# First block of a two-block model: norm statistics as rows from products with ones, and the first projections side by side

## The reference

```python
def rms_norm(x, g):
    xf = x.astype(jnp.float32)
    y = xf * lax.rsqrt(jnp.mean(xf * xf, axis=-1, keepdims=True) + EPS)
    return (y * g.astype(jnp.float32)).astype(x.dtype)

    for l in range(DEPTH):
        z = rms_norm(h, norm_g[l])
...
    zp = jnp.einsum('btd,de->bte', z, w_in)
```

## Time and profile before

| | us |
|---|---|
| median of 3 runs (lowest, highest) | 1664.25 (1663.14, 1668.55) |
| profiled execution, whole | 1667.13 |
| its span | 1665.3 |
| PE busy in it | 1588.7 |
| DVE busy | 1139.6 |
| ACT busy | 899.4 |
| mean granted clock of PE | 0.984 |

### The profile page before, as it was taken

How to read it: one execution, slowest core, us unless ns; L and a number is a source line. 1 busy time by engine, 2 the same in 40 slices (tenths; PEclk the granted TensorE clock), 3 DMA queues, 4 the chain that set the end, 5 groups by cost and what they waited for, 6 DMA issues and landing times.

```text
span 1665.3 us, 32288 instructions
## 1 busy us (share of the span) xinstructions
PE 1588.7 (95%) x12500; PEld 1539.7 (92%) x12500; DVE 1139.6 (68%) x1727; ACT 899.4 (54%) x1423; POOL 48.9 (3%) x60
## 2 busy tenths in 40 slices
PE   7989999997989999999999999999999999999996
PEld 7977899886888999999999999999999899999996
DVE  4875677458768766677877766676666786776666
ACT  5644565378665544467555544464445755464443
POOL 0000000000000000002100000000000030000000
PEclk9989999899999999999999999999999999999998
DMA  5433223544443655545445655556555544556554
GB/s 196 132 101 99 64 77 118 174 140 127 144 140 109 197 184 187 189 152 169 148 148 169 201 181 186 189 168 199 183 184 174 158 159 140 189 164 192 185 182 136
DMA packets 73314, 263.66 MB, mean 158 GB/s; under 512 B 8144, under 2 KB 9680, under 8 KB 73104
## 3 DMA queue, kind: packets, MB, share of 16 engines
q1 hardware_dynamic: 70560, 252.66, 47.4%
q0 software_dynamic: 2672, 9.86, 1.8%
HBM read 261.43 MB, written 1.05 MB: 158 GB/s over the span
## 4 chain that ended last, share of the span: by engine, by line
PE 82%; DVE 9%; ACT 5%; issue 2%; DMA 2%; DVEq 0%; SPq 0%; ACTq 0%
PE PS L1490 24%; PE PS L1492 23%; PE PS L1491 23%; DVE w_lo L944 3%; PE PS L1733 2%; PE PS L1676 1%; PE PS L1838 1%; DMA raw<-stream 1%; ACT w_hi L489 1%; DVE zf L1269 1%; PE PS L1501 1%; PE PS L1749 1%; PE PS L1666 1%; PE PS L1652 1%; ACT work L855 1%
## 5 line engine op out<-in xcount | busy, mean ns | idle before, releaser
L1490 PE MATMUL PS<-YH,w_hi 128*128 128x256 f32 (+1 forms) x2812 | 815.2, 290 | 19.0 <-DVE YL L1430 8.3
L1492 PE MATMUL PS<-YH,w_lo 128*128 128x256 f32 (+1 forms) x2812 | 799.9, 284 | 0.0
L1491 PE MATMUL PS<-YL,w_hi 128*128 128x256 f32 (+1 forms) x2812 | 799.5, 284 | 0.0
L944 DVE TENSOR_TENSOR w_lo<-raw,w_hi 128x1024 fp32r<-128x1024 f32 x476 | 585.6, 1233 | 167.2 <-ACT w_hi L489 163.9
L1490 PEld LDWEIGHTS PS<-YH,w_hi 128*128 128x128 f32 x2812 | 535.7, 191 | 27.3 <-issue 10.3
L489 ACT ACTIVATE w_hi<-raw 128x1024 fp32r<-128x1024 f32 x476 | 499.5, 1052 | 99.3 <-PE PS L1492 53.5
L1491 PEld LDWEIGHTS PS<-YL,w_hi 128*128 128x128 f32 x2812 | 535.7, 191 | 2.5 <-issue 0.5
L1492 PEld LDWEIGHTS PS<-YH,w_lo 128*128 128x128 f32 x2812 | 536.9, 191 | 0.0
L1490 PE MATMUL PS<-hH,w_hi 128*128 128x256 f32 x832 | 233.3, 280 | 6.4 <-DVE hL L1037 6.4
L1491 PE MATMUL PS<-hL,w_hi 128*128 128x256 f32 x832 | 233.3, 280 | 0.0
L1492 PE MATMUL PS<-hH,w_lo 128*128 128x256 f32 x832 | 233.3, 280 | 0.0
(11 more groups left out here) (296 smaller groups left out, 1414.8 us busy)
## 6 DMA issues: line engine op xcount, KB each, us to landing
raw<-stream SPq DMA_DIRECT2D x476, 512.0 KB, 4.1
work<-stream POOLq DMA_DIRECT2D x16, 512.0 KB, 4.1
X<-x SPq DMA_DIRECT2D x1, 1088.0 KB, 5.0
out<-zf SPq DMA_DIRECT2D x8, 128.0 KB, 2.0
work<-rope SPq DMA_DIRECT2D x1, 544.0 KB, 7.7
work<-levels POOLq DMA_DIRECT2D x1, 512.0 KB, 3.9
work<-inv_count POOLq DMA_DIRECT2D x1, 512.0 KB, 4.6
work<-band POOLq DMA_DIRECT2D x1, 408.0 KB, 4.6
```

The source lines that it names most:

```text
L944: dve.tensor_tensor(w_lo[:, s.slot, :], raw[:, s.slot % RAW, :], f32(w_hi[:, s.slot, :]), ALU.subtract).then_inc(lo_ready, 1)
L1490: pe.matmul(to, wh, xh, start=start, stop=False, skip_group_check=True)
L1491: pe.matmul(to, wh, xl, start=False, stop=False, skip_group_check=True)
L1492: return pe.matmul(to, wl, xh, start=False, stop=stop, skip_group_check=True)
```

## The change

In both norms of the first block, PE sums with ones as the stationary operand (128 x 128) and the squares as the moving one: 8 products of 272 columns, and every partition of bank 6 holds the row of sums. ACT takes the root straight from PSUM over 272 columns, with scale and epsilon in the same operation; DVE takes the reciprocal over 272 columns in `rsf`. The step of scale and epsilon, the diagonal and the spreading are gone. The dummy root stands ahead of the squares (at the start also ahead of the wait for x, and behind a new wait for the constants, since the root reads epsilon). At the start three slabs are split instead of two (`FIRST = 3`); ACT does its splits behind the root, and DVE does its own behind the reciprocal and ahead of the first `zf`, no longer ahead of the norm.

PE takes the first slabs side by side (`beside`): it waits for the last of them to be split, and then, chunk by chunk, issues the three matmuls of the chunk for each slab in its own bank. That holds for slabs 0 to 2 of the even layer and for the four `u` slabs of the odd layer's first group. `from_z` loses its wait for `zL`; its callers drop the argument.

```diff
--- before.py
+++ after.py
@@ -27,7 +27,7 @@
 RAW = 3
 LEAD = 4
 
-FIRST = 2
+FIRST = 3
 SLAB = 8 * P
 
 FF = 2816 // P
@@ -194,8 +194,7 @@
         hH = sb("hH", [P, 2, T1], F32R)
         hL = sb("hL", [P, 2, T1], F32R)
 
-        rs = sb("rs", [P, 3])
-        diag = sb("diag", [P, 3 * 96])
+        rsf = sb("rsf", [P, T1])
         ident = sb("ident", [P, P])
         C = sb("C", [P, ncols])
         ones = sb("ones", [P, P])
...
@@ -489,18 +483,18 @@
                 act.activation(w_hi[:, s.slot, :], raw[:, s.slot % RAW, :], ACT.Copy).then_inc(hi_ready, 1)
 
             def norm(v, xr, T, xo):
+                act.activation(warm[:, 1:2], warm[:, 0:1], ACT.Sqrt)
+                if xr is None:
+                    act.wait_ge(x_loaded, 16)
                 for c in range(DC):
                     if xr is not None:
                         act.wait_ge(x_ready, xr + c // 2 + 1)
                     act.activation(zf[:, c, 0:T], X[:, c, xo:xo + T], ACT.Square).then_inc(sq_ready, 1)
+                act.wait_ge(ssq_ready, v + 1)
+                act.activation(rsf[:, 0:T], PS[:, 6, 0:T], ACT.Sqrt, bias=eps_col, scale=1.0 / D).then_inc(root_ready, 1)
                 if xr is None:
                     for k in range(FIRST):
                         split(Slab(0, k))
-
-                act.activation(warm[:, 1:2], warm[:, 0:1], ACT.Sqrt)
-                act.wait_ge(ms_ready, v + 1)
-                w, n = tiles(T)
-                act.activation(rs[0:w, 0:n], rs[0:w, 0:n], ACT.Sqrt).then_inc(root_ready, 1)
 
             def norm_hi(v, T):
                 for c in range(DC):
@@ -914,7 +908,7 @@
                             split(odd(o_out(g - 1) + 3 + LEAD))
 
             act.wait_ge(warm_ready, 1)
-            act.wait_ge(x_loaded, 16)
+            act.wait_ge(consts, 4)
             norm(0, None, T1, 0)
             norm_hi(0, T1)
             for k in range(FIRST, LEAD):
@@ -945,15 +939,11 @@
                                   ALU.subtract).then_inc(lo_ready, 1)
 
             def norm(v, xr, T, xo, col):
-                dve.wait_ge(ssq_ready, v + 1)
-                w, n = tiles(T)
-                dve.tensor_scalar(rs[0:w, 0:n], PS[0:w, 6, 0:n], 1.0 / D, EPS, ALU.mult, ALU.add).then_inc(ms_ready, 1)
                 dve.wait_ge(root_ready, v + 1)
-                step.step(dve.reciprocal(rs[0:w, 0:n], rs[0:w, 0:n]))
-                dg = diag[0:w, 0:n * w].rearrange("p (n t) -> p n t", t=w)
-                dve.tensor_tensor(dg, ident[0:w, None, 0:w].to_broadcast([w, n, w]), rs[0:w, 0:n, None].to_broadcast([w, n, w]),
-                                  ALU.mult).then_inc(diag_ready, 1)
-                dve.wait_ge(spread_done, v + 1)
+                step.step(dve.reciprocal(rsf[:, 0:T], rsf[:, 0:T]))
+                if xr is None:
+                    for k in range(FIRST):
+                        split(Slab(0, k))
                 if xr is not None:
                     dve.wait_ge(x_ready, xr + 4)
 
@@ -962,7 +952,7 @@
                     dve.tensor_tensor(zL[:, c, 0:T], zf[:, c, 0:T], f32(zH[:, c, 0:T]), ALU.subtract).then_inc(zlo_ready, 1)
 
                 for c in range(DC):
-                    dve.scalar_tensor_tensor(zf[:, c, 0:T], X[:, c, xo:xo + T], C[:, bass.ds(col + c, 1)], PS[:, 6, 0:T],
+                    dve.scalar_tensor_tensor(zf[:, c, 0:T], X[:, c, xo:xo + T], C[:, bass.ds(col + c, 1)], rsf[:, 0:T],
                                              ALU.mult, ALU.mult).then_inc(zf_ready, 1)
                     if c:
                         low(c - 1)
@@ -1455,8 +1445,6 @@
                 for r in range(4):
                     scans(LAST, r)
 
-            for k in range(FIRST):
-                split(Slab(0, k))
             dve.wait_ge(x_loaded, 16)
             dve.wait_ge(p_loaded, 32)
             norm(0, None, T1, 0, C_N0)
@@ -1493,27 +1481,26 @@
 
             def norm(v, T):
 
-                w, n = tiles(T)
                 for c in range(DC):
                     pe.wait_ge(sq_ready, v * DC + c + 1)
-                    for t in range(n):
-                        m0 = min(t * w, T - w)
-                        last = pe.matmul(PS[0:w, 6, t:t + 1], zf[:, c, m0:m0 + w], ones[:, 0:1], start=(c == t == 0),
-                                         stop=(c == DC - 1), skip_group_check=True)
+                    last = pe.matmul(PS[:, 6, 0:T], ones[:], zf[:, c, 0:T], start=c == 0, stop=c == DC - 1)
                 last.then_inc(ssq_ready, 1)
-                pe.wait_ge(diag_ready, v + 1)
-                for t in range(n):
-                    m0 = min(t * w, T - w)
-                    last = pe.matmul(PS[:, 6, m0:m0 + w], ones[0:w, :], diag[0:w, t * w:(t + 1) * w], start=True, stop=True,
-                                     skip_group_check=True)
-                last.then_inc(spread_done, 1)
-
-            def from_z(s, to, v=None, T=T2, xo=0):
+
+            def beside(slabs, banks, v):
+
+                pe.wait_ge(lo_ready, slabs[-1].n + 1)
+                pe.wait_ge(root_ready, v + 1)
+                for k in range(DC):
+                    pe.wait_ge(zlo_ready, v * DC + k + 1)
+                    for s, to in zip(slabs, banks):
+                        last = mm3(to, s, k, zH[:, k, :], zL[:, k, :], k == 0, k == DC - 1)
+                        if k == DC - 1:
+                            last.then_inc(w_used, 1)
+
+            def from_z(s, to, T=T2, xo=0):
 
                 pe.wait_ge(lo_ready, s.n + 1)
                 for k in range(DC):
-                    if v is not None:
-                        pe.wait_ge(zlo_ready, v * DC + k + 1)
                     last = mm3(to, s, k, zH[:, k, xo:xo + T], zL[:, k, xo:xo + T], k == 0, k == DC - 1)
                 last.then_inc(w_used, 1)
                 return last
@@ -1546,8 +1533,9 @@
                 return pe.matmul(to, xl, wh, start=False, stop=stop, skip_group_check=True)
 
             def even_layer():
-                for i in range(6):
-                    from_z(even(i), job(i), 0 if i == 0 else None, T1)
+                beside([even(i) for i in range(FIRST)], [job(i) for i in range(FIRST)], 0)
+                for i in range(FIRST, 6):
+                    from_z(even(i), job(i), T1)
                 for c in range(5):
                     pe.wait_ge(csq_ready, c + 1)
                     last = pe.matmul(PS[:, c // 3, 0:T1], ones[:], csq[:, c, :], start=(c in (0, 3)), stop=(c in (2, 4)))
...
@@ -1737,8 +1725,11 @@
                         last.then_inc(whole_used, 1)
 
                 for g in range(GROUPS):
-                    for r in range(4):
-                        from_z(odd(o_u(g) + r), tile("u", 4 * g + r), 1 if g == r == 0 else None, T1)
+                    if g == 0:
+                        beside([odd(o_u(0) + r) for r in range(4)], [tile("u", r) for r in range(4)], 1)
+                    else:
+                        for r in range(4):
+                            from_z(odd(o_u(g) + r), tile("u", 4 * g + r), T1)
                     for r in range(4):
                         n = 4 * g + r
                         i = n // 2
...
```

More of the change, by code:

```diff
@@ L283, in program @@
         consts, warm_ready, zeroed = sem("consts"), sem("warm_ready"), sem("zeroed")
-        diag_ready, spread_done = sem("diag_ready"), sem("spread_done")
-        sq_ready, ssq_ready, ms_ready, root_ready = sem("sq_ready"), sem("ssq_ready"), sem("ms_ready"), sem("root_ready")
+        sq_ready, ssq_ready, root_ready = sem("sq_ready"), sem("ssq_ready"), sem("root_ready")
         zf_ready, zhi_ready, zlo_ready = sem("zf_ready"), sem("zhi_ready"), sem("zlo_ready")
@@ L467, in tree @@
             return v[:, :, 0, :], v[:, :, 1, :]
-        def tiles(T):
-            return (96, 3) if T == T1 else (P, T // P)
         def heads(buf, h):
@@ L1589, in even_layer @@
                 for i in range(2):
-                    from_z(even(E_KS + i), job(J_KS + i), None, T1)
+                    from_z(even(E_KS + i), job(J_KS + i), T1)
                     if i == 0:
@@ L1595, in swa_query @@
                 def swa_query(i):
-                    from_z(even(e_qs(i)), job(J_QS[i]), None, T1)
+                    from_z(even(e_qs(i)), job(J_QS[i]), T1)
                     units_at(e_qs(i))
@@ L1683, in even_layer @@
                         pe.wait_ge(gate_ready, n)
-                    from_z(even(E_G + n), PS[:, 7, 0:T1], None, T1)
+                    from_z(even(E_G + n), PS[:, 7, 0:T1], T1)
                     turned(n)
@@ L1750, in odd_layer @@
                                       start=True, stop=True, skip_group_check=True).then_inc(lru_done, 1)
-                        from_z(odd(o_gate(g) + r), tile("gate", n, 0, T2), None, T2, XO)
+                        from_z(odd(o_gate(g) + r), tile("gate", n, 0, T2), T2, XO)
                     if 0 < g < LAST:
```

## The result

| | before | after |
|---|---|---|
| median of 20 runs, us | 1666.22 | 1671.01 |
| lowest, highest | 1661.88, 1668.58 | 1666.54, 1673.36 |
| profiled execution's span | 1665.3 | 1667.8 |

What follows compares the result with a forecast made beforehand. TensorE (PE), busy 95% of the span, was taken as the bound. First norm +0.6 and second norm +6.5 gave +7.1 us on a median of 1664.25, so 1671.3; range 1665.0 to 1676.5.

Steps and rivals of the forecast that it cites:

- First norm: Start of the even layer, through its first three slabs: +0.6 us, bounds -0.9 and +2.1.
- the tail: Taps, splits and multiply-adds behind the odd layer's four slabs: the fourth tile is done 9.5 us after their end.
- The three splits on the path: First norm: three splits of weights on DVE between reciprocal and first zf, 3.50 us.
- The half clock of the slabs: Even layer's first three slabs: half clock loses 2.0 to 3.4 us, taken as 2.7.
- Second norm: Odd layer, from sums through the gate: +6.5 us; four slabs end 2.8 earlier, the gate starts 3.8 later.
- The chain behind the four: Behind the odd layer's four slabs, PE waits for all four tiles; the gate starts 9.55 us after the slabs.
- the clock behind it: Gate and next products behind the 9.5 us wait start at half clock: another 2.7 us (2.0 to 3.4).
- The sum: Whole kernel: +0.6 from the first norm and +6.5 from the second make +7.1 us, 1671.3.
- The clock stays up: Rival: full clock through the holes before and behind the odd layer's four slabs; 1666.0 us, chance 0.15.
- Swallowed waits: Rival: PE's waits in group 0 shrink by 2 us, first norm at its lower bound; +3.6, 1667.9, chance 0.15.
- Cycling through banks: Rival: changing bank after every third matmul makes PE pause and keeps the clock low; +20, 1684 us, chance 0.03.
- The tail is not waited for: Rival: the gate starts with the first tile, so the kernel is 2 us faster; chance 0.05.

Runs made afterwards that it cites:

- run 3: Changed kernel with the start's three splits moved: ACT's between squares and root, DVE's ahead of the norm; 1664.71 us, ratio to before 0.9988.
- run 6: Changed kernel plus small products of ones by ones on PE between the second norm's sums and the four slabs, and behind those slabs; 1667.46 us, ratio to before 1.0004.
- taps first: Changed kernel with the splits of slabs 5 to 7 behind all four taps and convolutions in the odd layer's group 0; 1672.49 us, again 1673.78.

## Why the prediction was right

**First norm, +0.6 forecast, -0.2 measured.** Squares at 5.76 (5.8), sums over at 12.6 (12.9), 6.04 us from sums to the first zf (6.0), first projection at 20.16 (20.5): the steps hold. The table load came off with 1.28 us. ACT's timeline of the kernel after shows it with its neighbour:

```profile
3.79 1.28 ACT L486 ACT_TABLE_LOAD   x1 [3.79 <-POOL fixed L424]
5.09 0.20 ACT L486 ACTIVATE warm<-warm 128x1 f32<-128x1 f32 x1
```

The dummy root starts 1.30 us after the load did, so the drain of 1.38 us that the Trainium skill adds (ScalarE: Activation LUTs, What ACT_TABLE_LOAD costs) isn't there; by it the whole would have come out 1.4 lower than forecast. Nor does it lie ahead of a load: in the tail a load starts at 345.17, right behind a tap, and the next operation at 346.46. The three splits on the path cost their whole 3.5 us (run 3). The half clock of the slabs (20.16 to 24.9) cost 2.4 us where 2.7 was taken.

**Second norm.** Sums 3.93 us (3.7), no fall of the clock in them; first projection 326.80 (326.7), the four slabs' end 341.25 (341.2), gate at 350.78 (350.75). The chain behind the four was the right one, and PE's waits for it are 5.5 us where more than 5 were asked for. The mis-sized term is **the clock behind it**: 2.7 was taken, the gate slab took 5.2 us instead of 3.0, which is 2.2. Run 6 shows that it is the tail that brings it, with 2.3 us.

**The sum.** 6.0 us at the second tile against 7.1 forecast, and 4.8 in the medians with an interval of 3.8 to 6.3. The measured value lies in the range. Of the 1.1 between forecast and trace, 0.8 are the first norm's and 0.5 the clock's; 0.3 goes the other way, because the even layer lost the first norm's small gain again (the second norm's sums start 0.06 later than before, not 0.2 earlier). What lies between 6.0 and 4.8 is within the interval. That 1671.01 came out 0.3 from the forecast 1671.3 is luck: the sum of 7.1 was 2.3 too large, and the base of 1664.25, from three runs, was 2.0 below the 1666.22 measured later.

**The rivals.** *The clock stays up* fell at both holes it named (0.50 from 326.8, 0.51 from 350.8), though run 6, where products hold the clock at both holes, comes near its time: 1667.5 against 1666.0. *Swallowed waits* fell: PE's 0.48 and 1.48 before the fourth products are there as before. *Cycling through banks* fell: in run 6, 98 records in 12.26 us, 0.125 each, at 1.00; so the rule of the Trainium skill (TensorE: Matmul & The Clock Gate, A second HAM failure mode: psum-queue depth-cycling) doesn't show in this kernel's order. *The tail is not waited for* fell with the four waits.

**What I read wrongly** is what I added in the runs: that DVE's splits were a removable part of the tail. They are the price of the next slabs, and moved back they return as a wait for a transfer, and often as a slow stretch behind it. The prediction had also taken one hole of 2.9 us with half clock behind it as the rule; over all traces such a hole had it in 20 of 39 cases. For its two holes the term held: behind the hole of 4.0 us and behind the tail, half clock followed in every trace that had no products there, if only briefly behind the shorter tail of taps first (0.79 and 0.81 over the gate slab in two of its traces).

## What to carry to other kernels

Work done side by side also ends together. Before four tiles are interleaved, ask what the first one released while the second was being made; here the interleaving saved 0.5 us (14.45 against 14.92 for the four slabs) and cost 6.5 in a consumer that had kept pace, and then the slow clock behind that hole. A step of a ring (split, release, next transfer) can only be moved later if the slab it calls for isn't due; and where the time of a hole is in question, taking the part away and adding it alone tells more than one profiled pair.

## What the runs showed of the hardware

Behind a hole of 2.9 us the clock fell in 20 of 39 cases, in kernels that differed nowhere near; behind the hole of 4.0 us it fell in all eight traces without products in it (0.62 to 0.76 over the 7 us behind it). The falls behind the three later holes come to 4.3 us in the profiled pair. Small products of ones by ones kept the clock at 1.00 through the hole of 4.0 us in all three kernels that had them there, and through the tail in both that had them in it (9.4 us, and 6.1 with taps first). In the traces they cost nothing, since they lay in time in which PE would have waited.

In the first norm, the sums start at half speed with a granted clock of 1.00, as the projections of the kernel before at 20 us did; eight took 6.29 us where at full clock five take 2.29. In these two places the granted clock misled, and the matmuls' spacing told the speed.
